# A decoder trunk's attention scores moved one stretch forward, and its loop units rounded and subtracted one step ahead

## The chip, the cores and the metric

One core of one Trainium2 chip runs the whole program in one launch. The metric is device time in microseconds (us) of that launch; lower is better. A core has a matrix engine (TensorE, PE in the rows), a vector engine (VectorE, DVE), a scalar engine (ScalarE, ACT), a general engine (GpSimd, POOL) and a queue for transfers (SyncE, SP). Each runs its own program in order, and they meet at semaphores only.

## What is computed

Two layers of a decoder over 256 tokens of width 1024. A layer is a gated feed-forward block, a mixer, and a second feed-forward block, each behind a norm and added to the residual `x`. The mixer is where the change lies:

```python
h = rms_norm(x, mix_norm[l])
(a_q, a_ckv, a_iq, a_ik, a_iw, b_u, c_q, c_kv_cmp, c_kv_sel, c_kv_win, c_gate, merge_gate) = jnp.split(h @ w_in[l], offsets, axis=-1)
y_a = dsa_mixer(...)    # keys chosen by an indexer's top-64, then attention
y_b = pool_mixer(...)   # trailing-window means, then a group product
y_c = nsa_mixer(...)    # gated sum of attention over compressed blocks, selected blocks and a window
g_a, g_b, g_c = jnp.split(jax.nn.sigmoid(merge_gate), 3, axis=-1)
merged = g_a * (y_a @ proj_a[l]) + g_b * (y_b @ proj_b[l]) + g_c * (y_c @ proj_c[l])
x = x + merged @ w_out[l]
```

The attention of `dsa_mixer` and `nsa_mixer` is scores, a mask, a softmax and a product with values, each for 8 heads and two tiles of 128 queries.

## The kernel before

**Weights.** All weights come as 198 units of 128 x 2048 numbers through a ring of three slots. SyncE loads a unit into `raw`; ScalarE rounds it into `whi` (`split`, L585, two halves by L579); VectorE subtracts to get the rest, `wlo` (`split`, L945, two halves by L960). TensorE forms each product as three: whi by xhi, wlo by xhi and whi by xlo (L1430 to L1432). Unit n takes the slot of unit n-3, so ScalarE waits at L591 until TensorE has counted unit n-3 as used, and VectorE waits at L949 for each rounded half.

**The mixer's input projection** runs in chunks of 512 columns, c from 0 to 11, for token tile 0 and then 1: chunk (c,0), chunk (c,1) (`chunk`, L1607), 24 products each. Chunk c uses units 2c-1 and 2c of the mixer, one in each half of the chunk. TensorE counts 2c-1 as used at the middle of chunk (c,1), and 2c at its end. Chunks 0 to 5 make keys, queries and values. Chunks 6 to 11 make the merge gates, in a loop of twelve steps, k = 0 to 11: step k is chunk (6 + k//2, k%2) and what stands behind it in the loop (L867 on ScalarE, L1308 on VectorE, L1805 on TensorE).

**Attention** is woven between the chunks in eleven batches, b = 0 to 10 (`BATCHES`, L86): selected blocks (sel), window (win), compressed blocks (cmp), and dsa, for query tile 0 or 1 and, with 256 keys, one half of the heads. For a batch, in this order:
- TensorE: `batch_scores(b)` (L1661) writes the banks SC once batch b-1 has been drained from them.
- VectorE: `mask_and_max(b)` (L1171, work at L1188, maxima at L1194) drains SC, adds the mask and finds row maxima.
- ScalarE: `exps(b)` (L751, work at L765) waits for the maxima and makes the exponentials.
- VectorE: `weigh(b)` (L1196, L1203 to L1216) waits for them, divides by the sums, applies the gates, turns the result.
- TensorE: `strip_values(n)` (L1674, work at L1707) multiplies a group of batches with the values, in the banks TO. `VALUES_AT` says in which steps the eight groups stand.

`LEAD` is how many batches the scores are ahead of the loop's step: step k issues the scores of batch k + LEAD.

Groups 0 to 2 sum the outputs of the first query tile; `split_o` takes them out of the banks in step 3, first rounded by ScalarE (L787), then the rest by VectorE (L1221). Group 3 starts to write the same banks anew, so TensorE waits for VectorE's part at L1686:

```python
if n in (3, 6):
    pe.wait_ge(o_drained, l * 4 + n // 3)
```

**Woven in as well**: eight rounds of the indexer's top-8 search (`topk_round`, L1150) and a `selection_bias` on VectorE; the key compression, whose first product is the turn `hid` (L1753), whose GELU goes over VectorE (L1277 to L1286) and ScalarE (L835), and whose end is the turn `cmpo`; the pooling's turns `band0`, `band1`, `yb0`, `yb1`; and GpSimd's rotation of queries and keys (`rope`, L478).

The order of all this is written out by hand, engine by engine.

Of the kernel before, what the change touches and what calls it, by code (L numbers as in the profile page):

```python
# [83 lines left out]


BATCHES = [  # L86
    ("sel", 0, 0), ("win", 0, 0), ("cmp", 0, 0),
    ("sel", 1, 0), ("sel", 1, 1), ("win", 1, 0), ("win", 1, 1), ("cmp", 1, 0),
    ("dsa", 0, 0), ("dsa", 1, 0), ("dsa", 1, 1)]
NB = len(BATCHES)  # L90
STRIP, STRIPS = 32, 4
CMP_W = 16


VALUE_GROUPS = [(0,), (1,), (2,), (3, 4), (5, 6), (7,), (8,), (9, 10)]
VALUES_AT = {2: (0, 1, 2), 4: (3,), 7: (4, 5), 10: (6, 7)}
GROUP_END = {("nsa", 0): 3, ("nsa", 1): 6, ("dsa", 0): 7, ("dsa", 1): 8}
NG = len(VALUE_GROUPS)
SLOT = {0: 0, 1: 1, 3: 2, 4: 3, 5: 0, 6: 1, 8: 2, 9: 0, 10: 1}
SLOT_FREE = {5: 1, 6: 2, 8: 4, 9: 5}  # L100
LEAD = 2
WARM_UP = 2
KEEP_WARM = 8
FIRST_GAINS = 24
# [21 lines left out]
def trunk(nc, x_in, pos_in, stream, small_in, w1_in, const_in, final_in, out):  # L126
    ctx = ExitStack()
    with ctx:
# [447 lines left out]
        def _(act):  # L576
# [8 lines left out]
            def split(l, at, u):  # L585
                n = at + u
                s = n % RING

                act.wait_ge(raw_in[s], (l * (LAYER_UNITS // RING) + n // RING + 1) * 16)

                act.wait_ge(unit_used, l * LAYER_UNITS + (n + 1))  # L591
                round_unit(s)
# [121 lines left out]
            def mixer(l):  # L714
                at = FFN_UNITS
                act.wait_ge(rstd_done, lift_of(l, 1) + 1)

                def drain_z(f):
                    c, tok = OPENING[f] if f < 4 else (f // 2, f % 2)
                    wait_g(act, l, f)  # L720
                    lo, hi = (0, C_S) if c == 0 else (C_S + (c - 1) * 512, C_S + c * 512)
                    act.activation(  # L722
                        z[:, tok, lo:hi], G[f % 2][:, 0 : hi - lo], ACT.Copy, scale=rs[:, tok : tok + 1]
                    ).then_inc(gz_drained, 1)
# [26 lines left out]
                def exps(b):  # L751
                    n, nh = keys_of(b), heads_of(b)
                    act.wait_ge(negmax_done, l * NB + b + 1)
                    if BATCHES[b][0] == "cmp":
                        w, p = CMP_W, cmp_probs
                    else:
                        w, p = n, probs[:, SLOT[b], :]
                    if b >= 2:

                        act.wait_ge(turned_probs, l * NB + b - 1)  # L760
                    if b in SLOT_FREE:

                        act.wait_ge(values_done, l * NG + SLOT_FREE[b])
                    for hh in range(nh):
                        ins = act.activation(  # L765
                            p[:, hh * w : hh * w + n], sm[:, hh * w : hh * w + n], ACT.Exp,
                            scale=0.125, bias=negmax[:, hh : hh + 1], accum_out=sums[b % 2][:, hh : hh + 1],
                        )
                    ins.then_inc(exp_done, 1)
# [13 lines left out]
                def split_o(branch, tok, dst, ks):  # L783

                    act.wait_ge(values_done, l * NG + GROUP_END[branch, tok])
                    col = P if (branch, tok) == ("dsa", 1) else 0
                    act.activation(by_strips(dst, ks, tok), strip_sums(col), ACT.Copy).then_inc(t_hi_done, 1)  # L787
# [46 lines left out]
                act.wait_ge(gelu_inner, l + 1)  # L834
                act.activation(hid_t, hid_t, ACT.Tanh, scale=0.7978845608028654).then_inc(gelu_tanh, 1)  # L835
                split(l, at, 11)
                drain_z(10)
                for j in range(2):
                    drain(
# [8 lines left out]
                        turn_bank("gelt")[:, ROWS + 16 * g : ROWS + 16 * (g + 1)].unsqueeze(1).to_broadcast([P, 8, 16]),  # L848
                        ACT.Copy)
                mark_drained(ins, "gelt")  # L850
                exps(0)
                split(l, at, 12)
                drain_z(11)
                act.wait_ge(t_filled, filled(l, "cmpo"))
                act.activation(
                    kcT[:, 0:N_CMP], turn_bank("cmpo")[:, 0:N_CMP], ACT.Copy, scale=0.5).then_inc(kc_done, 1)
                split(l, at, 13)
                exps(1)
                for j in range(2):
                    for g in range(2):  # L860
                        gg = 2 * j + g
                        ins = act.activation(
                            ybhi[:, gg, :], turn_bank(f"yb{j}")[:, g * S : (g + 1) * S], ACT.Copy,
                            scale=small[:, W_PSC + gg : W_PSC + gg + 1],
                        )
                    ins.then_inc(t_hi_done, 1)
                for k in range(12):  # L867
                    c, tok = Z_CHUNKS + k // 2, k % 2
                    if k not in (0, 2):
                        split(l, at, 2 * c + 1 + tok)  # L870
                    drain_gate(c, tok)
                    if k == 1:
                        split(l, at, 15)
                    if k == 0:
                        for j in range(2):
                            drain(
                                f"qd{j}", qdT[:, 2 * j : 2 * j + 2, :].rearrange("p a t -> p (a t)"),
                                turn_bank(f"qd{j}")[:, :],
                            )
                    if k in (3, 8):  # L880
                        split_o("nsa", k // 8, ychi, 0)
                    if k + LEAD < NB:
                        exps(k + LEAD)
                split(l, at, 25)
# [57 lines left out]
        def _(dve):  # L942
            steps = Steps(dve, dve_step)

            def split(l, at, u, *parts):  # L945
                n = at + u
                for part in parts or range(PARTS):

                    dve.wait_ge(hi_done, part_value(n, part, l * LAYER_UNITS))  # L949
                    subtract_hi(n % RING, part)  # L950
# [177 lines left out]
            def mixer(l):  # L1128
# [21 lines left out]
                def topk_round():  # L1150

                    for qt in range(2):
                        ins = dve.max(top8[:, qt, :], work[:, qt, 0 : P * (qt + 1)])
                    then(ins)
                    for qt in range(2):
                        w = work[:, qt, 0 : P * (qt + 1)]
                        ins = dve.match_replace(w, top8[:, qt, :], w, TAKEN)
                    then(ins)
# [59 lines left out]
                def split_o(n_hi, tok, dst_hi, dst_lo, ks, col=0):  # L1218

                    dve.wait_ge(t_hi_done, l * 10 + n_hi)  # L1220
                    dve.tensor_tensor(  # L1221
                        by_strips(dst_lo, ks, tok), strip_sums(col), by_strips(dst_hi, ks, tok).bitcast(F32), ALU.subtract
                    ).then_inc(o_drained, 1)
# [34 lines left out]
                for tok in range(TOKS):  # L1258
# [21 lines left out]
                then(dve.tensor_tensor(hid_t, hid_v, hid_v, ALU.mult))  # L1280
                then(dve.tensor_scalar(hid_t, hid_t, 0.044715, 1.0, ALU.mult, ALU.add))
                dve.tensor_tensor(hid_t, hid_t, hid_v, ALU.mult).then_inc(gelu_inner, 1)
                topk_round()
                split(l, at, 11)
                dve.wait_ge(gelu_tanh, l + 1)
                dve.scalar_tensor_tensor(hid_t, hid_t, 1.0, hid_v, ALU.add, ALU.mult).then_inc(gelu_done, 1)  # L1286
                mask_and_max(0)
                topk_round()
                topk_round()
                split(l, at, 12)  # L1290
                weigh(0)
                dve.wait_ge(kc_done, l + 1)
                own = const[:, K_OWN : K_OWN + 2].unsqueeze(2).to_broadcast([P, 2, HD])
                mark_drained(dve.tensor_tensor(
                    own_v, turn_bank("cmpo")[:, 64:192].rearrange("p (g d) -> p g d", g=2), own, ALU.mult), "cmpo")
                mask_and_max(1)
                split(l, at, 13)
                topk_round()
                for j in range(2):
                    dve.wait_ge(t_hi_done, l * 10 + j + 1)  # L1300
                    for g in range(2):
# [5 lines left out]
                    mark_drained(ins, f"yb{j}")  # L1307
                for k in range(12):  # L1308
                    c, tok = Z_CHUNKS + k // 2, k % 2
                    if k == 0:  # L1310
                        mask_and_max(LEAD)
                    if k + 1 < NB:
                        weigh(k + 1)
                    if k in (1, 3):
                        split(l, at, 2 * c + 1 + tok)
                    if k == 6:
                        topk_round()
                        selection_bias()
                    if k and k + LEAD < NB:
                        mask_and_max(k + LEAD)  # L1320
                    if k == 1:
                        split(l, at, 15)
                    if k > 3:
                        split(l, at, 2 * c + 1 + tok)
                    if k in (3, 8):
                        split_o(3 + k // 8, k // 8, ychi, yclo, 0)
                split(l, at, 25, 0)
                gated(0, 1, 0, 0)
                split(l, at, 25, 1)
# [97 lines left out]
        def _(pe):  # L1427
# [176 lines left out]
            def mixer(l):  # L1604
# [151 lines left out]
                for k in range(16):  # L1756
                    for y_ in range(2):
# [2 lines left out]
                            t[row : row + ROWS, 0:P], windows[:, y_, k, :, :].rearrange("p g n -> p (g n)"),  # L1760
                            w1[:, y_, k, :], start=k < 2, stop=k >= 14)
                ins.then_inc(t_filled, 1)
                chunk(5, 0)
                pe.wait_ge(const_in_sem, 16)
                pe.wait_ge(gz_drained, l * 24 + 10)
                for j in range(2):
# [7 lines left out]
                        ins = pe.matmul(t[:, g * S + P : (g + 1) * S], u[1], band[:, BAND0:BANDC], start=False,  # L1774
                                        stop=True, skip_group_check=True)
                    ins.then_inc(t_filled, 1)
                batch_scores(0)

                t = open_turn("gelt")
                pe.wait_ge(gelu_done, l + 1)  # L1780
# [20 lines left out]
                        t[:, 64 + g * HD : 64 + (g + 1) * HD], gelV[:, g * P : (g + 1) * P],  # L1801
                        small[:, W_W2 + HD : W_W2 + 2 * HD], start=True, stop=True)
                ins.then_inc(t_filled, 1)
                batch_scores(1)
                for k in range(12):  # L1805
                    c, tok = Z_CHUNKS + k // 2, k % 2
                    chunk(c, tok)
# [193 lines left out]
```

## Time and profile before

| what | us |
|---|---|
| median of three runs (1189.6 to 1189.79) | 1189.77 |
| the profiled execution | 1189.75 |
| its span, first to last instruction | 1187.9 |
| TensorE busy | 1175.4 |
| VectorE busy | 976.4 |
| ScalarE busy | 616.1 |
| GpSimd busy | 74.9 |

The first three are times of whole executions; the busy times are those of the one profiled execution, from its page. A product's end in the profile is modelled, so starts are the surer reading for TensorE. The mean granted TensorE clock was 0.998 of its full rate.

### The profile page before, as it was taken

How to read it: one execution, taken by the hardware profiler on the slowest of the kernel's cores; microseconds unless marked ns; L12 is line 12 of the kernel's file. 1: busy time of each engine (PE TensorE's matmuls, PEld its weight loads, DVE VectorE, ACT ScalarE, POOL GpSimd, SP SyncE). 2: the span in 40 equal slices, each digit the busy share in tenths (PEclk: the TensorE clock that was granted, in tenths of full speed). 3: DMA queues.
4: the chain of work that ended last, by engine and by line, in shares of the span. 5: the costliest groups of instructions: out<-in, count | busy, mean ns of one | idle time of the engine just before them, and what ended most of it. 6: DMA issues, size and time to landing. Idle time of an engine off the chain costs nothing.

```text
span 1187.9 us, 18888 instructions
## 1 busy us (share of the span) xinstructions
PE 1175.4 (99%) x6442; PEld 967.1 (81%) x6442; DVE 976.4 (82%) x2103; ACT 616.1 (52%) x1045; POOL 74.9 (6%) x151
## 2 busy tenths in 40 slices
PE   8999999999999999999999999999999999999997
PEld 7888888887778888888888888888877888888886
DVE  7988886678878698888788898875889696988886
ACT  6544446556654454444464444465566535444443
POOL 5300000421000000000000000024100000000000
PEclk9999999999999999999999999999999999999999
DMA  9655554553445465455565555535543554655553
GB/s 377 231 188 177 200 190 164 186 178 115 144 178 177 177 212 196 176 209 181 208 219 206 201 187 212 182 142 186 173 148 112 196 194 153 231 191 201 209 179 142
DMA packets 37143, 223.53 MB, mean 188 GB/s; under 512 B 6752, under 2 KB 9440, under 8 KB 11232
## 3 DMA queue, kind: packets, MB, share of 16 engines
q1 hardware_dynamic: 35360, 216.36, 51.4%
q10 hardware_dynamic: 1696, 6.43, 1.6%
q8 instruction: 35, 0.57, 0.2%
q14 instruction: 20, 0.16, 0.0%
q0 software_dynamic: 32, 0.00, 0.0%
HBM read 218.58 MB, written 1.05 MB: 185 GB/s over the span
## 4 chain that ended last, share of the span: by engine, by line
PE 86%; DVE 9%; ACT 3%; issue 2%; DMA 0%; DVEq 0%; ACTq 0%
PE G L1430 21%; PE G L1431 21%; PE G L1432 21%; DVE wlo L960 3%; PE TO L1432 3%; PE TO L1431 3%; PE TO L1430 3%; PE SC L1432 3%; PE SC L1431 3%; PE SC L1430 3%; ACT probs L765 2%; DVE sm L1188 1%; DVE probs L1215 1%; PE TO L1446 1%; PE TO L1707 1%
## 5 line engine op out<-in xcount | busy, mean ns | idle before, releaser
L960 DVE TENSOR_TENSOR wlo<-raw,whi 128x1024 fp32r<-128x1024 f32 x395 | 468.2, 1226 | 114.6 <-ACT whi L579 112.4
L579 ACT ACTIVATE whi<-raw 128x1024 fp32r<-128x1024 f32 x395 | 396.2, 1053 | 266.8 <-PE G L1432 149.2
L1430 PE MATMUL G<-whi,xhi 128*128 128x512 f32 x1184 | 464.4, 392 | 1.2 <-DVE wlo L1023 0.7
L1432 PE MATMUL G<-whi,xlo 128*128 128x512 f32 x1184 | 458.2, 387 | 0.0
L1431 PE MATMUL G<-wlo,xhi 128*128 128x512 f32 x1184 | 458.1, 387 | 0.0
L1430 PEld LDWEIGHTS G<-whi,xhi 128*128 128x128 f32 x1184 | 222.9, 188 | 54.4 <-issue 5.4
L1432 PEld LDWEIGHTS G<-whi,xlo 128*128 128x128 f32 x1184 | 222.8, 188 | 45.6
L1431 PEld LDWEIGHTS G<-wlo,xhi 128*128 128x128 f32 x1184 | 223.0, 188 | 43.3
L1054 DVE STREAM_TRANSPOSE shared_q<-shared_q 32x128 f32<-32x128 f32 x640 | 193.7, 303 | 8.3
L651 ACT ACTIVATE shared_q<-G,stat 128x256 f32<-128x256 f32 x88 | 41.8, 476 | 78.1 <-PE G L1432 75.5
L1430 PE MATMUL TO<-whi,ybhi 128*128 128x512 f32 x176 | 69.0, 392 | 0.0
L1430 PE MATMUL SC<-whi,ybhi 128*128 128x512 f32 x176 | 68.7, 390 | 0.0
L1432 PE MATMUL TO<-whi,yblo 128*128 128x512 f32 x176 | 68.5, 389 | 0.0
L1432 PE MATMUL SC<-whi,yblo 128*128 128x512 f32 x176 | 68.5, 389 | 0.0
L1431 PE MATMUL SC<-wlo,ybhi 128*128 128x512 f32 x176 | 68.5, 389 | 0.0
L1431 PE MATMUL TO<-wlo,ybhi 128*128 128x512 f32 x176 | 68.5, 389 | 0.0
L765 ACT ACTIVATE probs<-sm,stat 128x128 f32<-128x128 f32 (+1 forms) x96 | 42.5, 444 | 45.9 <-DVE stat L1194 45.9
L657 ACT ACTIVATE ybhi<-shared_q 128x512 fp32r<-128x512 f32 x40 | 25.3, 633 | 75.3 <-DVE shared_q L1054 75.3
L483 POOL TENSOR_TENSOR rot<-z,trig 128x64 f32<-128x64 f32 (+3 forms) x14 | 9.5, 677 | 760.9 <-ACT z L722 760.5
L1043 DVE SCALAR_TENSOR_TENSOR shared_q<-shared_q,stat,G 128x256 f32<-128x256 f32 x88 | 42.3, 481 | 3.1
L984 DVE SCALAR_TENSOR_TENSOR xlo<-TO,small,xhi 128x128 fp32r<-128x128 f32 x96 | 28.1, 343 | 16.2 <-ACT xhi L610 16.2
L1430 PEld LDWEIGHTS SC<-whi,ybhi 128*128 128x128 f32 x176 | 33.0, 188 | 6.9
(204 smaller groups left out, 968.5 us busy)
## 6 DMA issues: line engine op xcount, KB each, us to landing
raw<-stream SPq DMA_DIRECT2D x200, 1024.0 KB, 4.8
gates<-w_in ACTq DMA_DIRECT2D x2, 2048.0 KB, 8.6
z<-z SPq DMA_DIRECT2D x32, 64.0 KB, 4.2
x<-x_in SPq DMA_DIRECT2D x4, 256.0 KB, 5.8
raw<-stream SPq DMA_DIRECT2D x2, 512.0 KB, 5.7
small<-small_in ACTq DMA_DIRECT2D x2, 414.5 KB, 3.1
const<-const_in SPq DMA_DIRECT2D x1, 690.0 KB, 11.9
z<-zkv SPq DMA_DIRECT2D x32, 16.0 KB, 2.0
```

The source lines that it names most:

```text
L579: act.activation(whi[s][:, c], raw[s][:, c], ACT.Copy).then_inc(hi_done, 1)
L651: act.activation(tg[:, tok, :], G[tok][:, 0:FCH], ACT.Tanh, scale=rs_half[:, tok : tok + 1]).then_inc(tanh_done, 1)
L657: act.activation(hThi[j].rearrange("p k t -> p (k t)"), turned, ACT.Copy).then_inc(ht_hi_done, 1)
L765: ins = act.activation(p[:, hh * w : hh * w + n], sm[:, hh * w : hh * w + n], ACT.Exp, scale=0.125, bias=negmax[:, hh : hh + 1], accum_out ...
L960: dve.tensor_tensor(wlo[s][:, c], raw[s][:, c], whi[s][:, c].bitcast(F32), ALU.subtract).then_inc(lo_done, 1)
L984: dve.scalar_tensor_tensor(xlo[:, kt, sl], T[kt // 4][:, kt % 4 * P : (kt % 4 + 1) * P], small[:, g : g + 1], xhi[:, kt, sl].bitcast(F32), ...
L1043: dve.scalar_tensor_tensor(h[:, tok, :], h[:, tok, :], rs_sq[:, tok : tok + 1], G[tok][:, FCH : 2 * FCH], ALU.mult, ALU.mult).then_inc(h_d ...
L1054: ins = dve.transpose(turned[32 * c : 32 * c + 32, :, :, r, :], blocks[32 * r : 32 * r + 32, :, :, c, :])
L1188: ins = dve.tensor_tensor_reduce(sm[:, hh * w : hh * w + n], SC[hh % 2][:, (hh // 2) * n : (hh // 2 + 1) * n], bias, 1.0, -3.4e38, ALU.add ...
L1430: pe.matmul(o, ahi, bhi, start=first, stop=False)
L1431: pe.matmul(o, ahi, blo, start=False, stop=False)
L1432: return pe.matmul(o, alo, bhi, start=False, stop=last)
```

## The change

It reorders the batches (the compressed blocks of query tile 0 go from place 2 to place 3, behind a batch of selected blocks), sets `LEAD` to 3, and moves every batch's scores, mask, exponentials and weighing one stretch to the front: the first scores stand right behind `hid`, the second behind the bands, the third behind `cmpo`. In the loop, each engine's `split` of a unit stands one step earlier in number (unit 2c+2+tok in place of 2c+1+tok) and ahead of that step's `exps`. Two rounds of the top-8 search go into steps 1 and 2, the bias from step 6 to step 5. Value groups 4 and 5 go from step 7 to 6, groups 6 and 7 from step 10 to 9. The second `split_o` goes from step 8 to 7; the first stays in step 3.

```diff
 BATCHES = [
-    ("sel", 0, 0), ("win", 0, 0), ("cmp", 0, 0),
-    ("sel", 1, 0), ("sel", 1, 1), ("win", 1, 0), ("win", 1, 1), ("cmp", 1, 0),
+    ("sel", 0, 0), ("win", 0, 0), ("sel", 1, 0),
+    ("cmp", 0, 0), ("sel", 1, 1), ("win", 1, 0), ("win", 1, 1), ("cmp", 1, 0),
     ("dsa", 0, 0), ("dsa", 1, 0), ("dsa", 1, 1)]
-VALUE_GROUPS = [(0,), (1,), (2,), (3, 4), (5, 6), (7,), (8,), (9, 10)]
-VALUES_AT = {2: (0, 1, 2), 4: (3,), 7: (4, 5), 10: (6, 7)}
+VALUE_GROUPS = [(0,), (1,), (3,), (2, 4), (5, 6), (7,), (8,), (9, 10)]
+VALUES_AT = {2: (0, 1, 2), 4: (3,), 6: (4, 5), 9: (6, 7)}
-SLOT = {0: 0, 1: 1, 3: 2, 4: 3, 5: 0, 6: 1, 8: 2, 9: 0, 10: 1}
+SLOT = {0: 0, 1: 1, 2: 2, 4: 3, 5: 0, 6: 1, 8: 2, 9: 0, 10: 1}
-LEAD = 2
+LEAD = 3
...
                 split(l, at, 11)
+                exps(0)
                 drain_z(10)
...
-                exps(0)
                 split(l, at, 12)
+                exps(1)
                 drain_z(11)
...
                 split(l, at, 13)
-                exps(1)
...
+                exps(2)
                 for k in range(12):
                     c, tok = Z_CHUNKS + k // 2, k % 2
-                    if k not in (0, 2):
-                        split(l, at, 2 * c + 1 + tok)
                     drain_gate(c, tok)
-                    if k == 1:
-                        split(l, at, 15)
...
-                    if k in (3, 8):
-                        split_o("nsa", k // 8, ychi, 0)
+                    if k in (3, 7):
+                        split_o("nsa", k // 7, ychi, 0)
+                    if k < 11:
+                        split(l, at, 2 * c + 2 + tok)
                     if k + LEAD < NB:
                         exps(k + LEAD)
...
-                topk_round()
-                split(l, at, 11)
+                mask_and_max(0)
                 dve.wait_ge(gelu_tanh, l + 1)
                 dve.scalar_tensor_tensor(hid_t, hid_t, 1.0, hid_v, ALU.add, ALU.mult).then_inc(gelu_done, 1)
-                mask_and_max(0)
+                split(l, at, 11)
                 topk_round()
+                weigh(0)
+                mask_and_max(1)
                 topk_round()
                 split(l, at, 12)
-                weigh(0)
+                weigh(1)
...
-                mask_and_max(1)
+                mask_and_max(2)
                 split(l, at, 13)
-                topk_round()
...
                 for k in range(12):
                     c, tok = Z_CHUNKS + k // 2, k % 2
-                    if k == 0:
-                        mask_and_max(LEAD)
-                    if k + 1 < NB:
-                        weigh(k + 1)
-                    if k in (1, 3):
-                        split(l, at, 2 * c + 1 + tok)
-                    if k == 6:
+                    if k + 2 < NB:
+                        weigh(k + 2)
+                    if k == 5:
                         topk_round()
                         selection_bias()
-                    if k and k + LEAD < NB:
+                    if k + LEAD < NB:
                         mask_and_max(k + LEAD)
-                    if k == 1:
-                        split(l, at, 15)
-                    if k > 3:
-                        split(l, at, 2 * c + 1 + tok)
-                    if k in (3, 8):
-                        split_o(3 + k // 8, k // 8, ychi, yclo, 0)
+                    if k < 11:
+                        split(l, at, 2 * c + 2 + tok)
+                    if k in (1, 2):
+                        topk_round()
+                    if k in (3, 7):
+                        split_o(3 + k // 7, k // 7, ychi, yclo, 0)
...
                 ins.then_inc(t_filled, 1)
+                batch_scores(0)
                 chunk(5, 0)
...
-                batch_scores(0)
+                batch_scores(1)
...
-                batch_scores(1)
+                batch_scores(2)
                 for k in range(12):
```

## Rows read from the trace of the kernel before

**Rows 1.** The page, part 1: busy us, share of the span and instructions by engine.
```profile
PE 1175.4 (99%) x6442; PEld 967.1 (81%) x6442; DVE 976.4 (82%) x2103; ACT 616.1 (52%) x1045; POOL 74.9 (6%) x151
```
**Rows 2.** The page, part 4: the chain that ended last, by engine.
```profile
PE 86%; DVE 9%; ACT 3%; issue 2%; DMA 0%; DVEq 0%; ACTq 0%
```
**Rows 3.** Waits of TensorE: us in total, times, longest us.
```profile
PE G L1430 <- DVE wlo L960: 0.5, 2, 0.2
```
**Rows 4.** Timeline of TensorE around three late half units: start, us, instruction, idle before.
```profile
316.11 0.39 PE L1432 MATMUL G<-whi,xlo 128*128 128x512 f32 x1
316.73 0.50 PE L1430 MATMUL G<-whi,xhi 128*128 128x512 f32 x1 [0.24 <-DVE wlo L960]
317.07 0.39 PE L1431 MATMUL G<-wlo,xhi 128*128 128x512 f32 x1
...
332.37 0.39 PE L1432 MATMUL G<-whi,xlo 128*128 128x512 f32 x1
332.71 0.50 PE L1430 MATMUL G<-whi,xhi 128*128 128x512 f32 x1
...
344.78 0.39 PE L1432 MATMUL G<-whi,xlo 128*128 128x512 f32 x1
345.16 0.50 PE L1430 MATMUL G<-whi,xhi 128*128 128x512 f32 x1
```
**Rows 5.** Timeline of TensorE, start of chunk (7,1) to value group 3.
```profile
291.32 0.50 PE L1430 MATMUL G<-whi,xhi 128*128 128x512 f32 x1
...
303.17 0.39 PE L1431 MATMUL G<-wlo,xhi 128*128 128x512 f32 x1
303.40 0.39 PE L1432 MATMUL G<-whi,xlo 128*128 128x512 f32 x1
303.72 2.08 PE L1707 MATMUL TO<-probs,z 32*64 32x128 f32 x104
```
**Rows 6.** Stretch: us, busy PE, PEld, DVE, ACT, POOL; clock, DMA share, GB/s.
```profile
248.00:304.00 56.00, 56.00 (x463) 45.33 (x468) 47.21 (x160) 34.84 (x102) 4.01 (x4) 1.00 0.46 146
```
**Rows 7.** Timeline of VectorE: one top-8 round; mask, unit, weighing; output subtraction.
```profile
260.72 0.61 DVE L1153 MAX8 top<-work 128x8 f32<-128x128 f32 x2
...
262.15 0.62 DVE L1153 MAX8 top<-work 128x8 f32<-128x128 f32 x2
...
285.60 0.42 DVE L1188 CUSTOM_DVE_ANT_0 sm<-SC,const 128x256 f32<-128x256 f32 x1
...
287.17 2.35 DVE L960 TENSOR_TENSOR wlo<-raw,whi 128x1024 fp32r<-128x1024 f32 x2
289.44 0.17 DVE L1203 RECIPROCAL fac<-stat 128x4 f32<-128x4 f32 x1
...
292.28 0.42 DVE L1188 CUSTOM_DVE_ANT_0 sm<-SC,const 128x256 f32<-128x256 f32 x1
...
302.75 0.68 DVE L1221 TENSOR_TENSOR yclo<-TO,ychi 128x512 fp32r<-128x512 f32 x1
```
**Rows 8.** Timeline at chunk (4,1): its start, then the unit that waits for its middle.
```profile
242.56 0.48 PE L1430 MATMUL G<-whi,xhi 128*128 128x512 f32 x1
...
245.64 2.01 ACT L579 ACTIVATE whi<-raw 128x1024 fp32r<-128x1024 f32 x2 [2.01 <-PE G L1432]
...
246.80 2.36 DVE L960 TENSOR_TENSOR wlo<-raw,whi 128x1024 fp32r<-128x1024 f32 x2 [0.26 <-ACT whi L579]
```
**Rows 9.** Timeline of TensorE at the program's ends; granted clock after its last product.
```profile
8.81 0.77 PE L1430 MATMUL G<-whi,xhi 128*128 128x512 f32 x1 [0.71 <-DVE wlo L1023]
...
12.79 0.45 PE L1430 MATMUL G<-whi,xhi 128*128 128x512 f32 x1
...
1180.55 0.39 PE L1432 MATMUL TO<-whi,yblo 128*128 128x512 f32 x1
...
1183.75:1184.00 0.25, 0.00 (x0) 0.00 (x0) 0.21 (x2) 0.00 (x0) 0.00 (x0) 0.50 0.00 0
```

## The prediction

> **What bounds the kernel now.** I read the page first. TensorE is busy for 1175.4 us of a span of 1187.9 [rows 1], so at most 12.5 us of idle could be won anywhere, most of it before the first product and after the last. Then the chain of waits: 86% of it is TensorE, 9% VectorE and 3% ScalarE [rows 2]; the reader is to see that the other two engines stand on the path only in a few stretches. The largest such stretch is the one that the change edits. TensorE's own waits show how little is lost there: two waits on VectorE's subtraction, 0.2 us each, one per layer [rows 3].
>
> That view understates the loss, since a matmul's end is modelled and overlaps the next start, so I measured it from starts in TensorE's timeline. Neighbours in a run of 512-wide products start 0.23 us apart. In the merge-gate loop of layer 0 three gaps are longer with no other work between: 0.62 us before 316.73, 0.34 before 332.71, 0.38 before 345.16 [rows 4, 5]. After each the restart costs once more, 0.34 to the following start (317.07 shows it) instead of 0.23. So the three cost 0.50, 0.22 and 0.26, together **1.0 us**; all are the second half of an unsplit unit arriving late from VectorE. Layer 1 has the same three, and I count it the same: 2.0 us in all. VectorE has 47.21 us of work in the 56 us ahead of value group 3, so 8.8 us idle [rows 6].
>
> **The change part by part.** *Work.* No score, exponential, top-8 round (eight per layer still), rounding, subtraction or transfer is added or dropped, and no DMA is issued anywhere else in a queue; SP's unit loads follow the subtractions, which come no later until the loop. Cost 0 of itself. GpSimd's last rotation now begins about 2 us later, behind a delayed drain; the turn that needs it comes a whole chunk after that drain, so I cost it at nothing.
>
> *One break less.* A break in a chunk's stream by scores or values costs 0.32 instead of 0.23 on entry (303.40 to 303.72) [rows 5] and the restart's 0.34 instead of 0.23 on return: 0.2 us. Before, ten loop steps (0 to 8 and 10) have one; after, nine (0 to 7 and 9). The first scores go beside the key compression's product, where a break exists already. Gain **0.2 us** a layer.
>
> *Loop units earlier.* The unit rounded in step k now goes ahead of the exponentials of that step. For odd-numbered units it means up to a step more; for even ones the ring sets the time, since unit 2c+2 goes into the slot of unit 2c-1, which TensorE frees in the middle of chunk (c,1). The three late halves were units 18, 20 and 22. By adding up the same durations, they now come 2 to 4 us before they are needed. I take the whole 1.0 us a layer as gained.
>
> *All scores one step forward.* This is the term that costs. Value group 3, in step 4, may start only when VectorE has taken the pooled output of the first token tile out of its banks (the subtraction in split_o, end of step 3). That point stays in step 3, but VectorE must now also do one more weighing, one more mask-and-max and one more unit before it: 2.84 + 1.57 + 2.27 = 6.7 us [rows 7], while TensorE gets there only about 1 us later. The 8.8 us of idle would cover that if they could be used; one wait cannot be. In step 2 the subtraction of unit 16 needs its rounding, which needs unit 13's slot, free in the middle of chunk (7,1). So I count both engines from the start of chunk (7,1).
>
> TensorE: before, from that start (291.32) to value group 3 (303.72) come chunk (7,1), one score batch of 256 keys, and chunk (8,0) [rows 5]. After, the same three: **12.4 us**.
>
> VectorE: a freed slot's price is read at chunk (4,1), start 242.56: the rounding starts at 245.64, the subtraction at 246.80, **4.24 us** after the chunk's start [rows 8]. Then in program order: unit 16, 2.27 (287.17 to 289.44); a top-8 round, 1.43 (260.72 to 262.15); weighing batch 5, 2.84 (289.44 to 292.28); mask and max of batch 6, 1.57 (285.60 to 287.17); unit 17, 2.27; the output subtraction, 0.68 [rows 7]. Sum 11.06, end at **15.3 us**. ScalarE is done in time with its share (exponentials, first half of the output and unit 17 are all ready before VectorE asks).
>
> TensorE therefore stands still for 15.3 - 12.4 = **2.9 us**, once in each layer, before the first product of value group 3. Queued behind that wait on TensorE are group 3, score batch 7 and chunk (8,1), so everything after slips by it; nothing later has spare time to give back, as TensorE is full from there on. Before, VectorE finished the same subtraction at 303.43 for a start at 303.72 [rows 5, 7]: it was just in time already, which is why adding 6.7 us ahead of it shows.
>
> The next narrow place is VectorE's last weighing before groups 6 and 7. Laid out in the same way it is early by under 1 us. Below I bound a miss there by 0 and 1 us a layer and take 0.
>
> *Sum.* Per layer +2.9 - 1.0 - 0.2 = +1.7; two layers +3.4. The profiled execution took 1189.75 us (span 1187.9 and 1.85 around it), 0.02 under the median shown, so it needs no correction: 1189.75 + 3.4 = **1193.2 us**.
>
> *TensorE's clock.* After the last product of the program (start 1180.55) the granted clock stands at 0.50 from 1183.75, with no matmul between [rows 9]: that is the lower level, 1.2 GHz, reached after an idle stretch about as long as the one forecast. What a fall costs shows at the start, where products run at the lower level from 8.81 to 12.79: nine of them 0.44 us apart instead of 0.23, 1.9 us lost [rows 9]. The Trainium skill, TensorE: Matmul & The Clock Gate, "Why this matters for your kernels", warns of idle gaps between bursts of matmuls, since the clock then drops back to half. That speaks against this change, and by it the time would be that of rival C. The trace agrees for the program's end; no row here shows it within the mixer.
>
> **The rivals.** *B, not slower.* VectorE reaches the output subtraction before TensorE reaches group 3. Place: end of step 3. It decides at 12.4 us: VectorE's 15.3 would have to shrink by 2.9. For it: 8.8 us of idle exist in the stretch [rows 6]. Against: that idle lies ahead of the ring's wait, and the instructions behind the wait have the same durations wherever they stand in the timeline. It gives 1189.75 - 2 x 1.2 = 1187.4 us.
>
> *D, part of the wait.* The same place, with a stall of 0.6 to 2.4 us because a slot is freed or rounded earlier than at chunk (4,1). Net within 2.4 us over both layers: 1188.6 to 1192.1.
>
> *C, the clock falls too.* If the stall brings the lower level in one layer, 1193.2 + 1.9 = 1195.1; in both, 1197.0. The small products and scores that follow the stall may run slowly as well; I bound that by twice the price, 1200.8. For it: rows 9. Against: the forecast stall only just equals the idle stretch after which the level fell.
>
> **How the numbers follow.** The forecast (stall of about 2.9 us, clock held) 0.55; C 0.23; D 0.14; B 0.08. About 0.2%, 2.4 us, is what a measurement can tell from no change here. Slower is the forecast and C, 0.78; same is D, 0.14; faster is B, 0.08 (at 1187.4 it lies on the edge). The forecast's own range is 1192.2 to 1195.2: a stall 0.5 us shorter in each layer, or 1 us lost at groups 6 and 7. The full range goes from 1190.0, the middle of D, up to 1197.5, C with both layers at its lower price; it leaves out B, half of D and C's upper end, some 0.18.
>
> **What would show it.** Right: in each layer one TensorE idle of about 2.9 us before the first product into the output banks of value group 3, put down to VectorE's output subtraction; no gap over 0.23 us before the second halves of chunks (9,0), (10,0) and (11,0); VectorE waiting about 1.7 us on ScalarE's rounding of unit 16. Wrong: no such idle, or the three gaps still there, or the granted clock under 1.00 in the 5 us behind the stall (then C).

## The result and the profile after

The changed kernel took **1196.61 us** in the median of six executions (1193.38 to 1199.74), the kernel before 1189.68 beside it; the ratio is 1.0056 [1.0043, 1.0068]. It is slower, inside the range, and 3.4 us above the forecast of 1193.2. The profiled execution took 1193.74 us with a span of 1192.0, so it lies near the low end of the six; this decides how the miss is read further down.

The page of the changed kernel, parts 1 and 4 (busy time by engine; the chain that ended last):

```profile
PE 1173.7 (98%) x6442; PEld 968.1 (81%) x6442; DVE 976.1 (82%) x2103; ACT 615.7 (52%) x1045; POOL 73.1 (6%) x151
...
PE 96%; DVE 3%; ACT 1%; issue 0%; DMA 0%; ACTq 0%; DVEq 0%
```

The instruction counts are those of [rows 1]: nothing was added or dropped. The chain has become cleaner: VectorE's share fell from 9% to 3% [rows 2], because the stretches in which a unit came just in time are gone. Yet the kernel is slower. A share of the chain says how often another engine stands on the path, and not what one wait there costs. The waits of TensorE say that (us in total, times, longest us):

```profile
PE TO L1702 <- DVE yclo L1220: 6.0, 2, 3.0
PE SC L1868 <- DMA const<-const_in: 4.2, 1, 4.2
PE G L1425 <- DVE wlo L1022: 0.7, 1, 0.7
```

The row of [rows 3], waits on the mixer's `wlo`, is gone. In its place stands one wait of 3.0 us in each layer: value group 3 (L1702) on VectorE's output subtraction (L1220). The other two rows belong to the start of the program. TensorE's timeline of layer 0, from the start of chunk (7,1) over group 3 to the middle of chunk (9,0) (start, us, instruction, idle before):

```profile
292.79 0.50 PE L1425 MATMUL G<-whi,xhi 128*128 128x512 f32 x1
...
304.86 0.39 PE L1427 MATMUL G<-whi,xlo 128*128 128x512 f32 x1
308.23 2.08 PE L1702 MATMUL TO<-probs,z 32*64 32x128 f32 x104 [2.98 <-DVE yclo L1220]
310.24 1.07 PE L1651 MATMUL SC<-kcT,shared_q 64*128 64x15 f32 x16
...
320.62 0.39 PE L1427 MATMUL G<-whi,xlo 128*128 128x512 f32 x1
320.85 0.39 PE L1425 MATMUL G<-whi,xhi 128*128 128x512 f32 x1
```

Two things are to be seen. The last product before group 3 starts 12.07 us after the chunk's start, as in [rows 5] (303.40 - 291.32 = 12.08); then TensorE stands still. And the second half of chunk (9,0), at 320.85, follows its neighbour by 0.23 us, where before there was a gap of 0.62 [rows 4]. VectorE's side of the same stretch:

```profile
296.99 2.36 DVE L959 TENSOR_TENSOR wlo<-raw,whi 128x1024 fp32r<-128x1024 f32 x2 [1.49 <-ACT whi L579]
299.27 0.61 DVE L1152 MAX8 top<-work 128x8 f32<-128x128 f32 x2
...
300.70 0.18 DVE L1202 RECIPROCAL fac<-stat 128x4 f32<-128x4 f32 x1
...
303.55 0.42 DVE L1187 CUSTOM_DVE_ANT_0 sm<-SC,const 128x256 f32<-128x256 f32 x1
...
305.12 2.35 DVE L959 TENSOR_TENSOR wlo<-raw,whi 128x1024 fp32r<-128x1024 f32 x2
307.40 0.68 DVE L1220 TENSOR_TENSOR yclo<-TO,ychi 128x512 fp32r<-128x512 f32 x1
```

One instruction with a wait in front (1.49 us, unit 16 on its rounding), then an unbroken run: unit 16, a top-8 round, weighing, mask, unit 17, output subtraction. It ends at 308.08, that is 15.3 us after 292.79. The stretch as a whole (us; busy PE, PEld, DVE, ACT, POOL; clock, DMA share, GB/s):

```profile
248.00:310.00 62.00, 59.02 (x555) 47.72 (x556) 55.78 (x180) 40.23 (x117) 3.23 (x4) 1.00 0.47 149
```

VectorE is not full here: 55.78 of 62 us. TensorE lost its 3 us all the same, since the idle time lies ahead of the subtraction of unit 16 and the work behind it.

### The profile page after: what moved, and what is told of

Read it like the earlier page. It is cut to its first block, busy times and chain, and to the rows that moved or that the text cites. A ratio compares the mean times of both kernels' runs of the same rounds, so it can differ in the third digit from the quotient of the medians.

```text
span 1192.0 us, 18890 instructions
## 1 busy us (share of the span) xinstructions
PE 1173.7 (98%) x6442; PEld 968.1 (81%) x6442; DVE 976.1 (82%) x2103; ACT 615.7 (52%) x1045; POOL 73.1 (6%) x151
## 4 chain that ended last, share of the span: by engine, by line
PE 96%; DVE 3%; ACT 1%; issue 0%; DMA 0%; ACTq 0%; DVEq 0%
PE G L1425 24%; PE G L1426 23%; PE G L1427 23%; PE TO L1427 3%; PE TO L1426 3%; PE TO L1425 3%; PE SC L1426 3%; PE SC L1427 3%; PE SC L1425 3%; PE SC L1651 2%; PE TO L1702 2%; DVE wlo L959 1%; PE TO L1441 1%; PE TO L1641 1%; ACT whi L579 0%
## 5 line engine op out<-in xcount | busy, mean ns | idle before, releaser
L1427 PEld LDWEIGHTS TO<-whi,yblo 128*128 128x128 f32 x176 | 33.0, 188 | 6.9
```

The costliest lines, as they stand in the source:

```text
L1427: return pe.matmul(o, alo, bhi, start=False, stop=last)
```

## The experiments

Two theories stood against each other at first. **W**: the loss is the wait before value group 3, set by the place of one instruction in VectorE's order. **N**: so much was moved to the front that VectorE cannot follow, wherever its instructions stand. Beside them stood the question what the granted clock takes. The kernel before, run beside these, had medians of 1189.52 to 1189.87.

### The output subtraction ahead of the weighing

Changed kernel, one instruction moved: the first `split_o` goes to the head of step 3.

```diff
+                    if k == 3:
+                        split_o(3, 0, ychi, yclo, 0)
                     if k + 2 < NB:
                         weigh(k + 2)
...
-                    if k in (3, 7):
+                    if k == 7:
                         split_o(3 + k // 7, k // 7, ychi, yclo, 0)
```

> The changed kernel, with VectorE's output subtraction at the head of step 3 instead of its end; nothing added or dropped. Theory W (the whole loss is TensorE's wait for that subtraction): the wait of 3.0 us a layer is gone, what is left is the change's gain, so about 1187.5 us, below the kernel before (1189.7) and with runs within 0.5 us of each other. Rival N (VectorE has too much to do once the scores go forward, and the wait only moves to the next thing it is late with, score batch 7 or unit 17): TensorE waits elsewhere for most of the 3 us, 1190 us or more.

Measured: **1187.26 us** (1186.48 to 1188.01, 11 executions), ratio 0.9981 [0.9972, 0.999] to the kernel before. TensorE's waits, and then the same stretch by busy time:

```profile
PE SC L1870 <- DMA const<-const_in: 4.0, 1, 4.0
PE G L1427 <- DVE wlo L1022: 0.7, 1, 0.7
PE G L1427 <- DVE xlo L983: 0.5, 1, 0.5
```

```profile
248.00:310.00 62.00, 62.00 (x581) 50.52 (x578) 55.44 (x179) 40.17 (x116) 3.22 (x4) 1.00 0.45 145
```

No wait on the output subtraction is left, and TensorE is busy for all of the 62 us, with VectorE doing as much as in the changed kernel (55.44 against 55.78). The same work in another order: 9.4 us less in the median. N falls. This is faster than both kernels, by 2.3 us against the one before that ran beside it (1189.52), close to what the prediction counted as its gains (2 x 1.2).

### The output subtraction between mask and unit 17

```diff
                     if k + LEAD < NB:
                         mask_and_max(k + LEAD)
+                    if k == 3:
+                        split_o(3, 0, ychi, yclo, 0)
                     if k < 11:
                         split(l, at, 2 * c + 2 + tok)
```

> The changed kernel, with VectorE's output subtraction in step 3 between mask-and-max and the subtraction of unit 17. Theory W: the wait falls by exactly that unit, 3.0 - 2.27 = 0.7 us a layer, so 1187.5 + 2 x 0.7 = 1189.0 us, and the clock never falls. Rival N: the wait stays or moves, 1191 us or more.

Measured: 1188.93 us (1188.1 to 1189.36, 11 executions), ratio 0.9993 [0.9984, 1.0002]. TensorE at group 3:

```profile
305.84 2.08 PE L1704 MATMUL TO<-probs,z 32*64 32x128 f32 x104 [0.71 <-DVE yclo L1220]
```

The wait is 2.98 - 0.71 = 2.27 us shorter, which is one unit's subtraction (2.27 in the prediction). So the wait is as long as the instructions put ahead of the subtraction, minus a fixed allowance. Three points now lie on a line: 1187.26 with no wait; 1187.26 + 2 x 0.71 = 1188.7 against 1188.93 measured; 1187.26 + 2 x 2.98 = 1193.2 against the changed kernel's two lowest executions, 1193.38 and 1193.74. Its other four lie 3 to 6 us higher, and the wait does not explain that.

### The wait filled with other products

Changed kernel, with 12 extra products of 512 columns ahead of value group 3 in step 4, into a gate bank that the next chunk overwrites. The wait before group 3 stays; TensorE works while it lasts.

```diff
+                    if k == 4:
+                        pe.wait_ge(gz_drained, l * 24 + 16)
+                        for _ in range(12):
+                            pe.matmul(G[1][:, :], xhi[:, 0, 0:P], ..., start=True, stop=True)
                     for n in VALUES_AT.get(k, ()):
                         strip_values(n)
```

> The changed kernel, with twelve 512-wide products into a free bank put into TensorE's wait in each layer (they fill about 2.8 of its 3.1 us; their results are overwritten). Theory K (the runs above 1194 us are those in which TensorE's clock fell at the wait): every run at 1193.4 to 1194.0 us and a mean clock of 0.998. Rival (the spread is from elsewhere, transfers for one): as without them, 1193.4 to 1199.7 with a median near 1196.6.

Measured: 1193.94 us (1193.38 to 1194.03, 5 executions, mean granted clock 0.998 in each), ratio 1.0035 [1.0021, 1.0049].

```profile
305.05 2.88 PE L1811 MATMUL G<-xhi 128*128 128x512 f32 x12
308.19 2.08 PE L1702 MATMUL TO<-probs,z 32*64 32x128 f32 x104 [0.26 <-DVE yclo L1220]
```

Group 3 starts at 308.19, where it started at 308.23 without the filling: the extra products hide in the wait. But the spread over executions has gone from 6.4 us to 0.7, and all five have the clock of an undisturbed execution. The upper executions of the changed kernel are therefore TensorE's clock, and the idle time brings them.

### The wait made longer

The two top-8 rounds of steps 1 and 2 go to steps 2 and 3, so that one more stands ahead of the output subtraction.

```diff
-                    if k in (1, 2):
+                    if k in (2, 3):
                         topk_round()
```

> The changed kernel, with the top-8 round of step 1 put into step 3, ahead of the output subtraction; nothing added. Theory W: the wait grows by 1.43 to 4.4 us a layer, alone 1193.5 + 2.9 = 1196.4 us. Theory K on top of it: the clock falls in both layers of every run, 2 x 3.1 us more, 1202 to 1203 us with a clock of 0.992, and the profile shows the lower level behind the wait. If the falls have nothing to do with the length of the wait, the runs spread from 1196.4 to 1202.6 as they did before.

Measured: 1201.51 us (1201.16 to 1204.43, 4 executions, clock 0.993 in three and 0.991 in the slowest), ratio 1.0108 [1.0093, 1.0124]. The wait grew to 4.4 us per layer, as counted. By itself that gives 1187.26 + 2 x 4.4 = 1196.1; the other 5.4 us are put down to the clock, whose falls cost 3.9 and 1.3 us in the profiled execution, as read below. TensorE's timeline of layer 0, and then the granted clock (the third column from the right) by stretch in both layers:

```profile
309.27 3.72 PE L1702 MATMUL TO<-probs,z 32*64 32x128 f32 x104 [4.42 <-DVE yclo L1220]
312.92 1.89 PE L1651 MATMUL SC<-kcT,shared_q 64*128 64x15 f32 x16
314.74 0.79 PE L1425 MATMUL G<-whi,xhi 128*128 128x512 f32 x1
...
317.88 0.40 PE L1426 MATMUL G<-wlo,xhi 128*128 128x512 f32 x1
```

```profile
306.00:308.00 2.00, 0.00 (x0) 0.00 (x0) 1.97 (x7) 1.50 (x5) 0.00 (x0) 0.90 0.00 0
308.00:317.00 9.00, 7.73 (x125) 6.95 (x126) 4.81 (x25) 0.00 (x0) 0.00 (x0) 0.50 0.35 119
317.00:318.00 1.00, 1.00 (x4) 0.78 (x3) 0.00 (x0) 0.00 (x0) 0.00 (x0) 0.58 0.00 0
...
902.00:904.00 2.00, 2.00 (x77) 2.00 (x83) 1.93 (x3) 0.00 (x0) 0.00 (x0) 0.50 1.00 418
904.00:906.00 2.00, 2.00 (x54) 1.83 (x42) 0.67 (x1) 0.00 (x0) 0.00 (x0) 0.77 0.11 41
```

The clock falls to 0.50, 1.2 GHz, while TensorE stands still, and holds there for some 10 us in layer 0 and some 3 us in layer 1. What the fall costs is read from starts: group 3 to the scores 3.65 us instead of 2.01, scores to the first product 1.82 instead of 0.99, and seven steps of 0.43 to 0.59 instead of 0.23 to 0.34, 3.14 instead of 1.72. That is 1.6 + 0.8 + 1.4 = 3.9 us in layer 0. In layer 1 it is 1.3 us by the same reading, so a fall has no single price.

### The changed kernel once more

> The changed kernel itself once more, for more executions and perhaps a profile with a fall. Theory K: the executions fall into groups by their clock: 1193.4 to 1194 us at 0.998, about 3 us more for each layer with a fall (0.995), 6 us more with both (0.992).

Measured: 1196.71 us (1196.31 to 1198.06, 5 executions), ratio 1.0064 [1.0051, 1.0077]; the mean clock was 0.994 or 0.995 in each. Its profile has a fall in layer 1 and none in layer 0, with the same wait of 2.98 us in both. TensorE's timeline of layer 1, and the clock by stretch:

```profile
895.26 2.55 PE L1702 MATMUL TO<-probs,z 32*64 32x128 f32 x104 [2.98 <-DVE yclo L1220]
897.74 1.89 PE L1651 MATMUL SC<-kcT,shared_q 64*128 64x15 f32 x16
899.56 0.79 PE L1425 MATMUL G<-whi,xhi 128*128 128x512 f32 x1
...
903.56 0.40 PE L1425 MATMUL G<-whi,xhi 128*128 128x512 f32 x1
```

```profile
895.00:896.00 1.00, 0.74 (x51) 0.77 (x56) 0.93 (x4) 0.00 (x0) 0.00 (x0) 1.00 0.45 57
896.00:897.00 1.00, 1.00 (x67) 1.00 (x53) 0.97 (x2) 0.00 (x0) 0.00 (x0) 0.86 0.65 205
897.00:898.00 1.00, 1.00 (x16) 0.67 (x8) 0.94 (x1) 0.00 (x0) 0.00 (x0) 0.50 0.95 401
...
902.00:904.00 2.00, 2.00 (x7) 1.56 (x6) 0.00 (x0) 0.00 (x0) 0.00 (x0) 0.61 0.00 0
```

The level falls at about 896.7, some 1.4 us **after** the wait has ended, with TensorE at work again. The cost, by starts: 2.48 - 2.01, then 1.82 - 0.99, then 4.00 for eight products and one restart (903.56 - 899.56) that take 2.18 at full clock: 0.5 + 0.8 + 1.8 = **3.1 us**. That is the distance between the lower and middle executions of the changed kernel above (1196.6 - 1193.5). Three of the five fit theory K's middle group (1196.31 to 1196.71, clock 0.995). The two at 0.994 (1197.88 and 1198.06) lie between its groups, and none stayed undisturbed.

### The units alone, and the scores alone

Two kernels split the change. The first is the kernel before with only the loop's units one step ahead, on ScalarE and VectorE; scores, batches and value groups stay. VectorE's side of the diff:

```diff
...
-                    if k in (1, 3):
-                        split(l, at, 2 * c + 1 + tok)
...
-                    if k == 1:
-                        split(l, at, 15)
-                    if k > 3:
-                        split(l, at, 2 * c + 1 + tok)
+                    if k < 11:
+                        split(l, at, 2 * c + 2 + tok)
                     if k in (3, 8):
                         split_o(3 + k // 8, k // 8, ychi, yclo, 0)
```

> The kernel before with only the loop's units rounded and subtracted one step ahead; batches, lead and value groups as before. Theory W, by the same count: from the start of chunk (7,1) VectorE needs 4.24 + 2.27 + 2.84 + 1.57 + 2.27 + 0.68 = 13.9 us to the output subtraction's end, against TensorE's 12.4, so a wait of 1.5 us a layer, less the 1.0 us of the late halves: 1189.5 + 2 x 0.5 = 1190.5 us, and no fall of the clock. Rival U (units ahead are a pure gain, only the forward scores make the wait): no wait, 1187.5 us.

Measured: 1194.01 us (1191.98 to 1198.58, 6 executions, clock 0.993 to 0.999), ratio 1.0048 [1.0031, 1.0066]. TensorE at group 3 in the profiled execution (1191.98), and VectorE's waits from 286 to 308 us:

```profile
305.93 2.08 PE L1701 MATMUL TO<-probs,z 32*64 32x128 f32 x104 [2.18 <-DVE yclo L1219]
```

```profile
DVE wlo L958 <- ACT whi L579: 1.6, 1, 1.6
DVE fac L1201 <- ACT probs L765: 0.6, 1, 0.6
```

The wait is there without any score moved, so the units' half of the change brings most of it. It is 0.7 us longer than expected, and 0.6 of that is the second row: in this order the weighing waits for exponentials that stand behind unit 16's rounding on ScalarE, which the count had left out. The expectation of a steady clock failed too: three of the six executions have 0.996 or less and lie 3.4 to 6.6 us above the lowest, with a wait of only 2.18 us in the profiled one. The lowest, 1191.98 and 1192.00, are what the rows give by themselves: 1189.63 + 2 x (2.2 - 1.0) = 1192.0, since the three late halves are gone here too.

The second is the changed kernel with the units back in their old places, again with VectorE's side of the diff.

```diff
...
+                    if k in (1, 3):
+                        split(l, at, 2 * c + 1 + tok)
...
-                    if k < 11:
-                        split(l, at, 2 * c + 2 + tok)
+                    if k == 1:
+                        split(l, at, 15)
+                    if k > 3:
+                        split(l, at, 2 * c + 1 + tok)
```

> The changed kernel with the loop's units back at their old places; only the scores, their weighing and the value groups stand one stretch to the front. Theory W: unit 17 is no longer ahead of the output subtraction, so VectorE needs 4.24 + 2.27 + 1.57 + 0.68 = 8.8 us at most behind the ring and there is no wait; the second halves of units come late again; one break less is worth 0.4 us: 1189.2 us, between 1188.4 and 1190.2. Rival N (forward scores alone overload VectorE): a wait of over 1 us a layer at value group 3, 1191.5 us or more.

Measured: 1193.58 us (1193.15 to 1194.76, 5 executions), ratio 1.0032 [1.002, 1.0045]. TensorE's idle times around the loop's first half, layer 0:

```profile
303.46 0.50 PE L1431 MATMUL G<-whi,xhi 128*128 128x512 f32 x1 [0.26 <-DVE wlo L961]
306.87 2.08 PE L1708 MATMUL TO<-probs,z 32*64 32x128 f32 x104 [0.38 <-DVE yclo L1222]
321.39 0.50 PE L1431 MATMUL G<-whi,xhi 128*128 128x512 f32 x1 [1.75 <-DVE wlo L961]
```

The wait at group 3 is 0.4 us, where none was expected, and the time is 4.4 us above the 1189.2. It meets rival N's figure, but not its mechanism, a wait of over 1 us at group 3. Most of the loss is at unit 18, whose second half comes 1.75 us late. By starts, the late halves now cost 0.53 us (303.46, unit 16), 2.02 (321.39) and 0.23 (337.34, unit 20), 2.8 us a layer instead of 1.0. With the wait of 0.4 and 0.2 for the break less that makes 2.0 us a layer, and 4.0 in all is what was measured against the kernel before (1193.58 - 1189.63). Scores ahead without units ahead push work in front of a unit that was already late: of that work, the last top-8 round and the bias, which went from step 6 to step 5, take 2.5 us of VectorE just ahead of batch 8's mask and unit 18 (315.71 to 318.23).

### Units ahead and subtraction first, scores left alone

The first kernel of the pair above, and the subtraction at the head of step 3.

```diff
+                    if k == 3:
+                        split_o(3, 0, ychi, yclo, 0)
                     if k + 1 < NB:
                         weigh(k + 1)
...
-                    if k in (3, 8):
+                    if k == 8:
                         split_o(3 + k // 8, k // 8, ychi, yclo, 0)
```

> The kernel before with the loop's units one step ahead and the output subtraction at the head of step 3; the scores where they were. Theory W: no wait and no late halves, 1189.5 - 2.0 = 1187.5 us, so the forward scores are worth only the 0.4 us of a break. Rival: the forward scores are needed for the gain, and this one stays at 1188.5 us or more.

Measured: **1187.36 us** (1186.87 to 1187.84, 11 executions), ratio 0.9982 [0.9973, 0.9991]. TensorE at group 3:

```profile
302.77 0.39 PE L1428 MATMUL G<-whi,xlo 128*128 128x512 f32 x1
303.09 2.09 PE L1703 MATMUL TO<-probs,z 32*64 32x128 f32 x104
```

No wait. This kernel and the first experiment are 0.1 us apart, less than either spreads. So once the wait is out of the way, the units' move carries the gain, and the scores' move, first in the title of the change, is worth nothing that the times of whole executions can tell.

### The subtraction first, and nothing else

The control: the kernel before with the same move of the subtraction, units and scores untouched.

> The kernel before, with nothing changed but the place of the first output subtraction: it runs at the head of step 3, ahead of the weighing. Control for the two runs with this order that came out at about 1187.3 us. Theory W (the subtraction's place is worth only what a wait at value group 3 costs, and the kernel before has none there): no change within 0.2%, 1189.6 us, and no wait of TensorE on the subtraction, as in the kernel before. Rival O (the order alone carries the gain, by taking the subtraction out of the way of a unit's rounding behind it): 1187.4 us, and fewer late halves of units in the stretch of the loop's half units. Rival P (the subtraction ahead of the weighing now holds up unit 16's rounding, which is not yet one step ahead here): 0.2 to 0.7 us per layer slower, 1190.0 to 1191.0 us, with new waits on wlo behind value group 3.

Measured: **1197.48 us** (1196.98 to 1198.69, 5 executions), ratio 1.0064 [1.005, 1.0077]. All three expectations missed; the one that saw unit 16 held up had the mechanism, and a size several times too small. VectorE and TensorE in layer 0 (the row at 911.40 is layer 1), and the clock by stretch, layer 0:

```profile
299.19 0.69 DVE L1221 TENSOR_TENSOR yclo<-TO,ychi 128x512 fp32r<-128x512 f32 x1 [5.10 <-ACT ychi L787]
...
302.63 2.32 DVE L960 TENSOR_TENSOR wlo<-raw,whi 128x1024 fp32r<-128x1024 f32 x2
```

```profile
303.87 0.80 PE L1432 MATMUL G<-whi,xhi 128*128 128x512 f32 x1 [2.65 <-DVE wlo L960]
...
911.40 0.50 PE L1432 MATMUL G<-whi,xhi 128*128 128x512 f32 x1 [0.83 <-DVE wlo L960]
```

```profile
302.00:304.00 2.00, 0.13 (x1) 0.14 (x1) 2.00 (x3) 0.00 (x0) 0.00 (x0) 0.80 0.08 33
304.00:306.00 2.00, 2.00 (x5) 1.63 (x6) 2.00 (x9) 0.00 (x0) 0.00 (x0) 0.50 0.00 0
```

At the head of step 3 the subtraction waits 5.10 us for ScalarE's rounding of the output. Here unit 16 still stands behind it; its subtraction starts at 302.63 instead of 298.93, and TensorE waits 2.65 us for it in the second half of chunk (8,0), once per layer, with a fall of the clock in layer 0. In the two kernels at 1187.3 us unit 16 is already done by then, the wait of VectorE has shrunk to 0.37 and 1.61 us, and nothing urgent is queued behind it. So the two moves depend on each other: the units ahead alone cost 4.4 us in the median (1194.01 against 1189.63) and 2.4 in the lowest executions, the subtraction first alone costs 7.6 (1197.48 against 1189.87), and both together gain 2.3 (1187.36 against 1189.63). In the four other executions of this kernel the mean clock was 0.997 or 0.998, near an undisturbed one, and they are only about 1.4 us faster (1196.98 to 1197.78). Layer 1 of the profiled one, which has no fall, shows what they are made of: by starts the wait costs 2.9 us, and unit 18 comes late too (911.40, idle 0.83), 1.1 us instead of 0.50. That is 3.5 us a layer, and 1189.87 + 2 x 3.5 = 1196.9; up to 0.9 us of the four stays open.

## Why the prediction was right or wrong

**The wait before value group 3: right in place, cause and size.** Forecast 2.9 us per layer, measured 2.98. TensorE's side, 12.4 us, was 12.07 to the last product plus the usual 0.3. VectorE's side ended at 15.3, as forecast to the tenth: the slot's price was 4.20 us (296.99 - 292.79) against 4.24 [rows 8], and the durations of [rows 7] held in their new places. VectorE waited 1.49 us on the rounding of unit 16, named as about 1.7. That an engine had 8.8 us idle in the stretch [rows 6] helped nobody, as argued against rival B.

**The gains: right.** The three late halves are gone, and with the wait removed the first experiment comes out 2.3 us under the kernel before, against the predicted 2 x 1.2. How the 1.2 divides is less sure: the kernel with units ahead, subtraction first and scores left alone keeps all its breaks and gains the same within 0.1 us, so the 0.2 for a break was not seen in the times. By starts, from a product ahead of the loop to one behind it, the first experiment is 0.1 us shorter than that kernel in layer 0 and 0.2 in layer 1, about what was counted.

**Costs taken as nothing: right.** Groups 6 and 7 follow their chunk without a wait in the trace, and no new wait on GpSimd or on a transfer appears.

**The sum, against the execution that it was made for.** The span went from 1187.9 to 1192.0, by 4.1 us; 0.4 of it lies ahead of the mixer (the load of the constants, 4.2 us of wait instead of 4.0, and a slow start: products stand 0.43 us apart up to 13.44 instead of 12.79). The remaining 3.7 stand against 3.4. By starts the wait is 3.05 us (304.86 to 308.23, less the usual 0.32): group 3 starts 0.15 us after the subtraction's end, which the sum left out, 0.3 us for two layers.

**The step that failed: that the clock holds.** "The forecast stall only just equals the idle stretch after which the level fell" was put against rival C, with 0.23 for C and 0.55 for the held clock. The median lies outside the forecast's own range, 1192.2 to 1195.2, and inside the full range only because that one was drawn out to C; so the hit is C's more than the forecast's. (Two bounds of that range are rough: the middle of D is 1190.4 and C with both layers at its lower price 1197.0, where 1190.0 and 1197.5 stand. Nothing hangs on it.) The clock went the other way: four of six executions of the changed kernel, and all five of the repeat, show a lower mean clock. The prediction's own sign of it, a clock under 1.00 within 5 us behind the stall, is there in layer 1 of the repeat.

C named the mechanism, and its price, 1.9 to 3.8 us per fall, holds the 3.1 read in the repeat and nearly the 3.9 of the longer wait, while the 1.3 in layer 1 there lies below it. (The profile's clock column shows 1.00 at the program's start, where the price was read; that the lower level ran there was inferred from products 0.44 us apart. In the falls traced since, at 0.50, they stand 0.42 to 0.43 apart, which bears it out.) The median of 1196.6 fits the wait plus one fall of 3.1. Filling the wait with products takes the falls away, which shows that idle time is their cause; and with a wait of 2.18 us three executions of six already show a lower mean clock, though the one that was profiled is not among them.

The weight was wrong because one row at the program's end was read as the point below which nothing happens. The same event stands in every trace, and it varies. The last product and the clock behind it, with the scores alone, and then in the first experiment:

```profile
1185.59 0.39 PE L1433 MATMUL TO<-whi,yblo 128*128 128x512 f32 x1
1188.25:1188.50 0.25, 0.00 (x0) 0.00 (x0) 0.20 (x2) 0.00 (x0) 0.00 (x0) 0.57 0.00 0
...
1177.75 0.39 PE L1429 MATMUL TO<-whi,yblo 128*128 128x512 f32 x1
1182.50:1182.75 0.25, 0.00 (x0) 0.00 (x0) 0.00 (x0) 0.00 (x0) 0.00 (x0) 0.95 0.00 0
```

From the last product's start to the fall it is 2.7 us in the one and 5.0 in the other, 3.1 in the kernel before; in the mixer of the control (subtraction first, nothing else) it was 2.4 (300.83 to 303.2). A single reading of 3.1 gave no limit.

What the Trainium skill, TensorE: Matmul & The Clock Gate, "Why this matters for your kernels", says of idle gaps between bursts of matmuls, that the clock then drops back to half, thus decides the median here. The repeat agrees (0.50 from 897 us on). The first profile of the changed kernel, with the same wait and a clock of 1.00 throughout, shows that a gap of this length does not always do it.

## What to carry to other kernels

When work is moved forward on an engine that runs in order, look for the short instruction behind it that sets a buffer free for the bound engine: here 0.7 us of work at the wrong place cost 3 us a layer, twice, and its right place is behind the last thing it would hold up and ahead of everything that can wait. Count both engines from the last event that they share (here the release of a ring slot), since idle time ahead of that event is worth nothing. And give an idle stretch of TensorE like those here (2.18 us was the shortest that came with a lower mean clock) a second price, for the clock, with a chance of its own.

## What the runs showed of the hardware

The granted clock fell in some executions and not in others of the same kernel with the same wait: 2.98 us of idle time brought a fall in layer 1 of the repeat and none in layer 0, and none in either layer of the first profile; 2.65 us brought one in layer 0 of the control and none in layer 1. The 1.75 us with the scores alone brought none in the trace: its mean clock of 0.997 comes from a fall at the program's start (10.7 us), and its other four executions have 0.998 or 0.999. The fall came up to 1.7 us before TensorE's next product (307.6 against 309.27 with the longer wait), or 1.4 us after it had started again. The lower level then lasted from some 3 to some 10 us and cost 1.3 to 3.9 us. Why one wait brings it and its equal does not stays open: no run here set the moment of the wait by itself.
